# One section for the retention, banded and latent mixers of a hybrid layer, with operations over all token tiles and the query norms in the score scale

## The reference

```
# retention: 4 heads of 64, rope on q and k, decay mask D_h
s = (rope(q) @ rope(k).T) * D_h            # masked to earlier chunks
o = s @ v
y_ret = silu(g) * (o - mean(o)) / sqrt(var(o) + eps)      # per head
# banded attention with sinks: 4 query heads, 2 key heads of 64
q, k = rope(rms(q) * g_q), rope(rms(k) * g_k)
y_swa = softmax([q @ k.T * 64**-0.5 in the band, sink])[:-1] @ v
# latent attention: ranks 192 and 128, heads of 64 + 32 (rope part)
q = (rms(c_q) * g_cq) @ w_uq;  k_nope, v = (rms(c_kv) * g_ckv) @ w_ukv
q = rope_tail(rms(q) * g_qn);  k = rope_tail(rms([k_nope, k_rope]) * g_kn)
y_mla = softmax(q @ k.T * 96**-0.5, causal by chunk) @ v
```

## Time and profile before

| | us |
|---|---|
| runs shown: median of 3 (lowest, highest) | 4570.27 (4560.54, 4576.37) |
| the profiled execution, own time | 4590.38 |
| its span from first to last instruction | 4588.6 |
| first instruction of `retention` to the first of the attention units, layer 1 | 111.7 |
| the same, layer 2 | 111.2 |
| the attention units, layer 1 | 78 |

### The profile page before, as it was taken

One profiled execution on the slowest core, in us unless ns is written; L12 is line 12 of the kernel. 1 busy time (PEld: TensorE's weight loads), 2 busy tenths in 40 slices (PEclk: granted clock), 3 DMA queues, 4 the chain that ended last, 5 costly groups with the idle time before them and its releaser, 6 DMA issues. The chain is left out here.

```text
span 4588.6 us, 57827 instructions
## 1 busy us (share of the span) xinstructions
PE 4222.3 (92%) x18760; PEld 3429.6 (75%) x18760; DVE 2641.5 (58%) x5180; ACT 1499.2 (33%) x2689; POOL 2143.8 (47%) x1384
## 2 busy tenths in 40 slices
PE   7868799999999999999978588899999999999999
PEld 5446677778888788888864466778787887888887
DVE  6654430787676555555576634308866864555554
ACT  3123333334343322222231233333343433222222
POOL 7431434456465544444373315235564655444443
PEclk9957899999999999999989578999999999999999
DMA  3001313474655766666420013134756648666664
GB/s 108 26 11 42 110 56 112 150 205 146 199 175 172 232 206 193 192 195 193 139 94 21 11 44 117 60 120 142 207 162 179 193 153 252 193 194 192 196 192 138
DMA packets 504918, 656.69 MB, mean 143 GB/s; under 512 B 293856, under 2 KB 299104, under 8 KB 501600
## 3 DMA queue, kind: packets, MB, share of 16 engines
q1 hardware_dynamic: 203616, 519.45, 35.7%
q10 hardware_dynamic: 301056, 134.24, 10.6%
HBM read 508.88 MB, written 144.70 MB: 142 GB/s over the span
## 5 line engine op out<-in xcount | busy, mean ns | idle before, releaser
L1791 DVE TENSOR_TENSOR t_hots<-t_stages,t_hots 128x512 fp32r<-128x512 f32 x256 | 620.8, 2425 | 605.4 <-ACT t_hots L1605 605.4
L1644 POOL TENSOR_TENSOR t_ul<-t_u,t_uh 128x1024 fp32r<-128x1024 f32 x252 | 614.0, 2437 | 580.0 <-ACT t_uh L1546 580.0
L1816 PE MATMUL bank<-h_high,t_uh 128*128 128x512 f32 x2048 | 807.0, 394 | 29.8 <-POOL t_ul L1644 16.1
L1816 PE MATMUL bank<-h_low,t_uh 128*128 128x512 f32 x2048 | 804.8, 393 | 0.0
L1816 PE MATMUL bank<-h_high,t_ul 128*128 128x512 f32 x2048 | 801.2, 391 | 0.0
L1858 PE MATMUL bank<-t_v_early,t_hots 128*128 128x512 f32 x3072 | 711.4, 391 | 12.4 <-DVE t_hots L1791 12.4
L1858 PE MATMUL bank<-h_high,t_hots 128*128 128x512 f32 x3072 | 706.7, 389 | 0.0
L1858 PEld LDWEIGHTS bank<-t_v_early,t_hots 128*128 128x128 f32 x3072 | 579.7, 189 | 134.1 <-DVE t_hots L1791 13.3
L1858 PEld LDWEIGHTS bank<-h_high,t_hots 128*128 128x128 f32 x3072 | 576.6, 188 | 119.7
L1661 POOL TENSOR_TENSOR t_v_early<-t_stages,t_v_early 128x1024 fp32r<-128x1024 f32 x128 | 306.6, 2396 | 392.1 <-ACT t_v_early L1601 392.1
L1661 POOL TENSOR_TENSOR h_high<-t_stages,h_high 128x1024 fp32r<-128x1024 f32 x128 | 307.9, 2406 | 380.8 <-ACT h_high L1601 380.8
(11 more groups left out here) (392 smaller groups left out, 6369.0 us busy)
## 6 DMA issues: line engine op xcount, KB each, us to landing
t_u<-in_peer_u SPq DMA_DIRECT2D x256, 512.0 KB, 3.6
t_stages<-in_peer_v SPq DMA_DIRECT2D x256, 512.0 KB, 4.1
acts<-t_act ACTq DMA_DIRECT2D x256, 256.0 KB, 3.0
gates<-t_stages ACTq DMA_DIRECT2D x128, 512.0 KB, 5.4
t_stages<-acts SPq DMA_DIRECT2D x256, 256.0 KB, 4.3
t_stages<-gates SPq DMA_DIRECT2D x256, 256.0 KB, 4.5
p_w_raw<-in_peer_wq SPq DMA_DIRECT2D x64, 256.0 KB, 3.1
m_w_raw<-in_w_in SPq DMA_DIRECT2D x48, 256.0 KB, 2.6
```

Source lines behind the costliest of these rows:

```text
L1644: e.tensor_tensor(ul[:, n % 2, :, :], u[:, n % 2, :, :], uh[:, n % 2, :, :].bitcast(F32), ALU.subtract).then_inc(u_split, 1)
L1791: e.tensor_tensor(al[:, s, :], a_in[:, s, :], ah[:, s, :].bitcast(F32), ALU.subtract).then_inc(act_split, 1)
L1816: mm = e.matmul(k.bank[n % 2][:, :], a[:, n % 2, q, :], b[:, q, :], start=(q == 0 and m == 0), stop=(q == KT - 1 and m == 2))
```

## The change

`retention` and `window_and_latent` become one function and one section, `mixers`. One barrier per layer goes. PE's order is: latent transposes, up-projections (J_UP), retention transposes (J_RT), retention scores (J_RS), transposes of the banded heads (J_WIN), retention values (J_RV), transposes of the latent heads (J_FULL), attention. DVE's order is: latent statistics, retention rotation, latent gains, banded heads, statistics and queries of the latent heads, keys scaled, 16 masks, keys finished, normalisation of retention, attention. POOL has no work left in the section. The squares go to ACT (with a running sum for the latent rows, from PSUM for the heads). Operations that ran once per tile cover all four tiles. The norm of a query is no longer multiplied into it: it goes with the constant of the scores into a column per head (wqs, mqs), which L357's operation takes as its scalar in place of a number. The three masks are loaded behind the weights. The rings of the attention share memory with r_sm, and the tiles of the section aren't padded to 256 bytes.

```diff
+def mixers(k, z, y):
...
+    J_LAT, J_UP, J_RT, J_RS, J_WIN, J_RV, J_FULL, base = 0, 3, 11, 19, 35, 41, 45, 53
+    owners = ["V"] * 3 + ["A"] * 16 + ["V"] * 16 + ["A"] * 18
...
+        shared = sb("shared", [P, NH * sum(widths)])
+        sm = shared[:, :].rearrange("p (h w) -> p h w", h=NH)
+        s_ring, p_ring, pt_ring = (shared[:, n * RING * SEQ:(n + 1) * RING * SEQ].rearrange("p (r w) -> p r w", r=RING) for n in range(3))
...
+                    [(wT[:, h, t * P:(t + 1) * P], wT[:, 4 + kvh, lo * P:(t + 1) * P])], nk, wqs[:, t, h:h + 1],
...
+                    [(mT[:, h, t * P:(t + 1) * P], mT[:, NH + h, 0:(t + 1) * P])], t + 1, mqs[:, NH * t + h:NH * t + h + 1],
...
+        def turn_heads(e, done, tl, x):
...
+            x1, x2 = x[:, :, :, HD:HD + HALF], x[:, :, :, HD + HALF:MD]
+            cc, ss = (bcast(f[:, :, :].rearrange("p t (d two) -> p t d two", two=2)[:, :, :, 0], 2, NH) for f in (k.cos, k.sin))
+            for n, (u, v) in enumerate(((x1, cc), (x2, ss), (x1, ss), (x2, cc))):
+                e.tensor_tensor(turns[:, n, :, :, :], u, v, ALU.mult).then_inc(done, tl.one())
...
+            e.tensor_tensor(x1, turns[:, 0, :, :, :], turns[:, 1, :, :, :], ALU.subtract).then_inc(done, tl.one())
+            e.tensor_tensor(x2, turns[:, 2, :, :, :], turns[:, 3, :, :, :], ALU.add).then_inc(done, tl.one())
...
-                e.tensor_tensor(qk[:, :, :, :].rearrange("p t h d -> p t (h d)"), wz, wz, ALU.mult).then_inc(squares_made, 1)
...
-                    e.tensor_tensor(qk[:, t, :, :], qk[:, t, :, :], gw[:, :].rearrange("p (h d) -> p h d", h=NW), ALU.mult).then_inc(pool, tl.one())
...
-                    rotate(e, pool, tl, o[:, :, 0, :], o[:, :, 1, :], v[:, :, 0, :], v[:, :, 1, :],
...
-                for t in range(POOL_KEYS):
-                    keys_of(e, pool, tl, t, t1, t2)
-                e.sem_inc(keys_ready)
...
+                e.dma_start(mask_r[:, :, :], k.i["c_ret"]).then_inc(m_loaded, 16)
+                e.dma_start(mask_w[:, :], k.i["c_window"]).then_inc(m_loaded, 16)
+                e.dma_start(mask_m[:, :], k.i["c_causal"]).then_inc(m_loaded, 16)
...
-                    e.tensor_tensor(sq[:, t, 0:320], z[:, t, C_CQ:C_KR], z[:, t, C_CQ:C_KR], ALU.mult).then_inc(done, tl.one())
...
-                e.tensor_reduce(lst[:, 0:TT], sq[:, :, 0:Q_RANK], AX.X, ALU.add).then_inc(done, tl.one())
...
+                e.wait_ge(lat_squared, 2 * TT)
...
                 e.wait_ge(squares_made, 1)
...
+                e.tensor_reduce(st[:, :, :].rearrange("p t h -> p (t h)"), qr[:, :, :, :].rearrange("p t h d -> p (t h) d"), AX.X,
+                                ALU.add).then_inc(done, tl.one())
...
+                    e.tensor_scalar(lat[:, t, 0:Q_RANK], z[:, t, C_CQ:C_CKV], lrs[:, t:t + 1], None, ALU.mult).then_inc(lat_ready, 1)
...
+                rotate(e, done, tl, o_[:, :, :, 0, :], o_[:, :, :, 1, :], x[:, :, :, 0, :], x[:, :, :, 1, :],
+                       bcast(k.cos[:, :, :], 2, 8), bcast(k.sin[:, :, :], 2, 8), t1[:, :, :, :], t2[:, :, :, :])
+                e.sem_inc(rows_ready)
...
                 for n, (r, col) in enumerate(((P, 0), (HD, 1), (P, 0))):
...
                     e.tensor_scalar(latT[0:r, n, :], k.bank[n][0:r, :], gain, None, ALU.mult).then_inc(vector_freed, 1)
...
+                e.tensor_tensor(qk[:, :, :, :].rearrange("p t h d -> p t (h d)"), wz, bcast(gw[:, :], 1, TT), ALU.mult).then_inc(done, tl.one())
+                e.wait_ge(rooted, 2)
+                e.reciprocal(st[:, :, :], st[:, :, :]).then_inc(done, tl.one())
+                settle()
+                e.tensor_tensor(qk[:, :, NH:NW, :], qk[:, :, NH:NW, :], bcast(st[:, :, NH:NW], 3, HD), ALU.mult).then_inc(done, tl.one())
+                e.tensor_scalar(wqs[:, :, :], st[:, :, 0:NH], HD ** -0.5, None, ALU.mult).then_inc(done, tl.one())
...
+                rotate(e, done, tl, o_[:, :, :, 0, :], o_[:, :, :, 1, :], x[:, :, :, 0, :], x[:, :, :, 1, :],
+                       bcast(k.cos[:, :, :], 2, NW), bcast(k.sin[:, :, :], 2, NW), t1[:, :, 0:NW, :], t2[:, :, 0:NW, :])
+                e.sem_inc(win_ready)
...
+                e.tensor_tensor(kr[:, :, :], z[:, :, C_KR:], z[:, :, C_KR:], ALU.mult).then_inc(done, tl.one())
...
                 e.wait_ge(scalar_freed, 8)
...
                 e.tensor_reduce(hst[:, 0:16], kf[:, :, :, :].rearrange("p t h d -> p (t h) d"), AX.X, ALU.add).then_inc(done, tl.one())
...
+                e.tensor_reduce(hst[:, 16:32], cen[:, :, :], AX.X, ALU.add).then_inc(done, tl.one())
...
+                e.tensor_tensor(every, every, bcast(gq[:, :], 1, TT * NH), ALU.mult).then_inc(done, tl.one())
+                settle()
+                turn_heads(e, done, tl, mq)
+                settle()
+                e.sem_inc(q_ready)
...
-                for t in range(TT):
-                    e.tensor_tensor(mq[:, t, :, :], mq[:, t, :, :], bcast(hrs[:, 4 * t:4 * t + 4], 2, MD), ALU.mult).then_inc(done, tl.one())
-                    e.wait_ge(done, tl.n)
-                    finish_heads(e, done, tl, mq, t, gq[:, :], t3, t4)
...
+                e.reciprocal(hrs[:, :], hst[:, :]).then_inc(done, tl.one())
+                settle()
+                e.tensor_scalar(mqs[:, :], hrs[:, 0:16], MD ** -0.5, None, ALU.mult).then_inc(done, tl.one())
+                rk = hrs[:, 16:32].rearrange("p (t h) -> p t h", t=TT)
+                e.tensor_tensor(kf[:, :, :, 0:HD], kn, bcast(rk, 3, HD), ALU.mult).then_inc(done, tl.one())
+                e.tensor_tensor(kf[:, :, :, HD:MD], bcast(z[:, :, C_KR:], 2, NH), bcast(rk, 3, ROPE), ALU.mult).then_inc(done, tl.one())
...
+                e.wait_ge(m_loaded, 48)
+                for n in range(J_RS, J_RS + 16):
+                    h, j = (n - J_RS) // TT, (n - J_RS) % TT
+                    e.wait_ge(pe_jobs, n + 1)
+                    e.tensor_tensor(sm[:, h, starts[j]:starts[j] + widths[j]], k.bank[n % 8][:, 0:widths[j]],
+                                    mask_r[:, h, 0:widths[j]], ALU.mult).then_inc(vector_freed, 1)
...
+                e.tensor_tensor(every, every, bcast(gk[:, :], 1, TT * NH), ALU.mult).then_inc(done, tl.one())
...
+                turn_heads(e, done, tl, kf)
...
+                e.sem_inc(keys_ready)
...
+                e.wait_ge(scalar_freed, 16 + 6 + 4)
+                e.tensor_reduce(mu[:, :], o[:, :, :], AX.X, ALU.add).then_inc(done, tl.one())
...
+                e.wait_ge(rooted, 4)
+                e.reciprocal(rs[:, :], var[:, :]).then_inc(done, tl.one())
...
+                e.tensor_tensor(sq[:, :, :], cen[:, :, :], bcast(rs[:, :], 2, HD), ALU.mult).then_inc(done, tl.one())
...
+                for t in range(TT):
+                    e.activation(sq[:, 0:3, :].rearrange("p a d -> p (a d)"), z[:, t, C_CQ:C_CKV], ACT.Square,
+                                 accum_out=lst[:, t:t + 1]).then_inc(lat_squared, 1)
...
+                e.activation(qr[:, :, :, :].rearrange("p t h d -> p t (h d)"), wz, ACT.Square).then_inc(squares_made, 1)
...
+                e.activation(sg[:, :, :], z[:, :, C_RG:C_RG + GW], ACT.Silu).then_inc(silu_ready, 1)
...
+                        src = k.bank[n % 8][:, 0:NH * MD].rearrange("p (h d) -> p h d", h=NH)
+                        e.activation(mq[:, t, :, :], src, ACT.Copy)
+                        e.activation(kf[:, t, :, :], src, ACT.Square).then_inc(scalar_freed, 1)
...
+                        e.activation(kv[:, t, :], k.bank[n % 8][:, :], ACT.Copy)
+                        src = k.bank[n % 8][:, :].rearrange("p (h two d) -> p h two d", two=2, h=NH)[:, :, 0, :]
+                        e.activation(cen[:, NH * t:NH * (t + 1), :], src, ACT.Square).then_inc(scalar_freed, 1)
...
+                e.wait_ge(to_root, 4)
+                e.activation(var[:, :], var[:, :], ACT.Sqrt).then_inc(rooted, 1)
...
+                e.wait_ge(rows_ready, 1)
+                for n in range(J_RT, J_RS):
+                    bank_free(e, n, owners, freed)
+                    transpose_job(e, k.bank[n % 8], [rot[:, t, n - J_RT, :] for t in range(TT)], k.ident[:, :], pe_jobs)
+                for n in range(J_RS, J_WIN):
+                    h, j = (n - J_RS) // TT, (n - J_RS) % TT
+                    bank_free(e, n, owners, freed)
...
                 e.wait_ge(win_ready, 1)
-                for n in range(11, 17):
...
+                    transpose_job(e, k.bank[n % 8], [qr[:, t, n - J_WIN, :] for t in range(TT)], k.ident[:, :], pe_jobs)
+                for n in range(J_RV, J_FULL):
+                    t = n - J_RV
...
+                    e.wait_ge(vector_freed, 19)
...
-                retention(k, z, y)
-                window_and_latent(k, z, y)
+                mixers(k, z, y)
```

More of the change, by code:

```diff
@@ L789, in window_and_latent @@
[L789 to L796 removed]
+    NW, HALF = 6, ROPE // 2
     with ExitStack() as c:
         def sb(name, shape, dt=F32):
[L799 removed]
+            return k.sb("a_" + name, shape, dt, ctx=c, filled=False)
@@ L909, in _, with settle @@
                 done = vec
```

(47 more changed lines are left out.)

243 lines of the change are left out of this document (63 added, 180 removed).

## The result

The changed kernel takes 4504.85 us (median of 4 runs, 4495.39 to 4517.63), the kernel before, beside it on the same chip, 4572.85 (median of 4 runs, 4560.54 to 4576.37). The ratio is 0.9849 with a 95% interval of 0.9833 to 0.9865: 68.0 us less by the medians, where 65.4 were forecast (4505). All runs used here were in the fast state but one of the kernel before in the first group of experiments (15165.46 us at a granted clock of 0.318), which no median or ratio here takes in.

What follows compares the result with a forecast made beforehand. Bound: a chain through DVE and PE, which take turns. Eleven steps sum to 79.0 us against 111.7 per layer, 32.7 less; twice that is 65.4, and 4570.3 - 65.4 = 4504.9, say 4505; range 4486 to 4538.

Steps and rivals of the forecast that it cites:

- step 9: Sixteen retention masks on DVE, 6.9 us, to S + 50.7 (S: section's start); PE's remaining scores at 0.59 each.
- step 10: Retention values on PE, 15.1 us, to S + 69.2; DVE finishes the keys under them, then waits about 14 us.
- Steps 1 to 4: Latent squares on ACT, DVE's reduction and scalings, retention rotation (7.3 us), three latent gains: done at S + 18.9.
- Step 5: Up-projections, 24 matmuls, 14.1 us, to S + 33.0; DVE's banded heads lie under them.
- Steps 6 to 8: Last copy, square and reductions, queries over all tiles, keys scaled: from S + 33.0 to S + 43.8.
- the clock gives part back: Rival: scores and up-projections at the low clock, 33.4 us saved instead of 65.4, 4537 us; chance 0.13.
- the clock rises further: Rival: retention values and first half of up-projections run faster, 81.4 us saved, 4489 us; chance 0.06.
- lower end of 11.0: Retention values at the pace of their first 4.0 us: 11.0 us instead of 15.1.
- Step 11: ACT's copy, retention's mean, variance, root and normalisation: root at S + 76.2, about 1 us late; first unit at S + 79.0.
- The two new table loads: ACT's table loads for roots, at S + 5.2 and near S + 39: 1.28 us each, nothing added to the path.
- The column operand: L357's scalar from a column: at most 0.04 us per operation, 1.3 us per layer; taken as 0.
- Attention: Attention of both layers unchanged, longer than 78 us being a sign of error; rival of slower attention, chance 0.05.

Runs made afterwards that it cites:

- e_pool: Changed kernel with the banded heads' gain product, key scaling and rotation given back to POOL: 4513.03 us, ratio 0.9870.
- e_serial: Changed kernel with all its new operations, but retention finished before the latent part begins: 4529.12 us, ratio 0.9906.
- e_norm_in: Changed kernel with query norms multiplied into the queries again and L357's constant back as its scalar: 4527.26 us, ratio 0.9895.
- e_att_fill: Changed kernel with the 16 masks ahead of the queries, plus one idle matmul before each attention score matmul: 4500.99 us, ratio 0.9855.
- e_masks_filler: Changed kernel with the 16 masks ahead of the queries and thirteen idle matmuls before the up-projections: 4481.44 us, ratio 0.9791.
- e_filler: Changed kernel with six idle matmuls on PE before the up-projections: 4506.90 us, ratio 0.9864.
- e_masks_first: Changed kernel with DVE's 16 masks moved ahead of the queries and the keys' scaling: 4485.71 us, ratio 0.9800.
- e_filler_long: Changed kernel with thirteen idle matmuls on PE before the up-projections: 4495.74 us, ratio 0.9826.

## Why the prediction came out right, and where its terms were wrong

The mechanism was right: the overlap came about, DVE's wait in the up-projections was 5.03 (about 5 forecast), and the first L357 came at S + 73.2, against 79.0. The one wait on the path that was mis-sized is PE's within the scores (step 9). The total hit better than the terms did, by luck. The traces gave 82.4 us where 65.4 were forecast: 75.4 in the preparation (10.0 over, since the clock gave more in step 10 than it took in step 9), 4.0 in the attention and 3.0 outside the mixers, both put at nothing. The medians gave 68.0, and that 4504.85 lies so near 4505 is also because the median of before came out 2.6 higher than the one that the forecast started from.

- *Steps 1 to 4* were right within 1.1 us: the gains were done at S + 17.9 (18.9). The rotation took 7.3, by six operations of 1.23.
- *Step 5*, 14.1 us, was 13.1; its clock rose a little sooner than that of before. That the banded heads would be covered was right (e_pool). *Steps 6 to 8*, 10.8, were 10.5: S + 41.6.
- *Step 9* is one of the two terms that were mis-sized: 10.0 us in place of 6.9. I had seen that DVE would meet full banks, and costed the refill at the full clock. But PE was done with its first eight scores at S + 39.1, 4.0 ahead of the forecast (43.1), the masks came at S + 41.6, and after a pause of 3.25 us, forecast as under 1, the other scores ran at 0.50. This was the rival "the clock gives part back", at 3.1 us where it had 8.3 for all sixteen scores: since the steps before were shorter, the masks were done 0.9 us later than forecast, the banded transposes 1.4.
- *Step 10* is the other: 15.1 us forecast at today's clock, 9.0 measured at 1.00. This is 6.1 per layer, in the direction of the rival "the clock rises further", and beyond its lower end of 11.0, which was taken from a stretch that itself was at 0.81 (the prediction's first paragraph has the values at 0.50 to 0.54 throughout, which isn't what the earlier trace rows show). The reason given for staying with 0.50, that it fell there with PE busy throughout, was a fact of one trace, and not of the matmuls: they took 9.04 us in both layers of all nine kernels with the new order, and in e_serial, with the old one, 15.47 and 9.12. DVE's idle time there was 9.35, not 14.
- *Step 11* was 5.9 us from the values to the root in place of 7.0. The transposes of the latent heads took 3.8, not 6.2, again by the clock, so ACT's copies were done in time and the root was not late: DVE was the last. The two new table loads were hidden, as forecast. The second began at 242.00, and its root at 243.29, 1.29 us later, as for the load and the Silu in the earlier trace rows. The drain that the Trainium skill (ScalarE: Activation LUTs, What ACT_TABLE_LOAD costs) adds to a load doesn't show here either.
- *The column operand.* Its bound of 0.04 was too low: it is 0.06, and an L357 operation went above 0.74, which I had named as a sign of being wrong. The value that I took, 0, held: PE bounds the attention (e_norm_in). The bound came from an operation of another kernel part with other operands.
- *Attention* was forecast unchanged; it was 78.3 and 72.8; the first is over 78, another sign that I had named, by 0.3. Over all these kernels but e_att_fill, with nearly the same instructions, it ranges from 72.8 to 82.4, and the two layers of one execution can differ by 8 (82.4 and 74.3 in e_masks_filler, 74.3 and 82.4 in e_serial). The granted clock is what moves: mean 0.64 in the short one of layer 2. So a comparison of single executions carries some 5 us per layer of this, and the medians are to be trusted over it.

What follows for the better version: masks first and thirteen idle matmuls bring 4481.44 (ratio 0.9791), masks first alone 4485.71 (0.9800), both below the changed kernel's 4504.85 (0.9849).

## What to carry to other kernels

After an overlap is written, look again at which engine waits at each hand-over: here a block of 16 operations behind 6 us of work that nobody was waiting for held PE up for 3.25 us, and the low clock that followed cost more than the wait (4.4 us in the scores, 1.5 in the transposes). When engines take turns, first ask what each turn costs: 26.7 of 38.4 us and 30.6 of 36.9 were there without the overlap, from operations that were fewer, wider, dropped or moved off POOL, with 3.7 and 9.7 us of clock in that. How much each of these kinds brought was told apart for the wide operations (5.7 and 4.7 us) and the query norms (about 2) alone. And price a matmul stage at both clocks, for the level in an old trace is that trace's: e_serial had both in its two layers.

## What the runs showed of the hardware that was not expected

- The same 80 value matmuls took 15.1 us at 0.50 to 0.81 in before and 9.04 at 1.00 in after, with PE busy throughout in both; in e_serial, behind the same work, 15.47 in layer 1 and 9.12 in layer 2. What keeps the clock low in a busy stretch (the first 40 us of attention, 38.9 busy, at 0.50) these runs don't tell.
- A pause of PE was followed by the low clock, at once or within 1 us, in each such case here: 3.25 us (scores, after), 3.90 (e_filler), 5.29 (attention, after) and 6.74 (up-projections, after, where it had been low before too). Without the pause the same scores (e_masks_first) and up-projections (e_filler_long) ran at 1.00.
- A scalar from a column adds 0.06 us to an operation on PSUM, at each width measured: 0.692 to 0.751 at 512 columns, 0.558 to 0.618 at 384, 0.424 to 0.484 at 256.
- A DVE operation of 24 columns lasted 1.54 us beside one of POOL (e_pool), and 0.18 without (after).
- The granted clock rose from 0.50 to 1.00 while PE did nothing but transposes, after a pause of 11.96 us (before, 216.41 to 221.83, mean 0.67).
